# Gate matrices from two accumulated rounded products with a split gate value, and reordered joints in a hybrid attention and PEER block

## The reference

```python
xn = rms_norm(h); proj = xn @ w_in            # q, k, v of two branches, two gates
y_a = sliding_window_sink_attention(...)      # softmax whose denominator is sum(p) + exp(sink - m)
y_b = chunked_relbias_attention(...)
h += (sigmoid(g_a) * (y_a @ w_a) + sigmoid(g_b) * (y_b @ w_b)) @ w_out
# PEER: 8 heads, 128 + 128 sub-keys, 16 experts of 16384 for each head
qry = rms_norm(h) @ w_query
s1, s2 = qry[half 0] @ keys1.T, qry[half 1] @ keys2.T
v1, i1 = top_k(s1, 16); v2, i2 = top_k(s2, 16)
top_s, pos = top_k(all 256 sums v1 + v2, 16); idx = i1 * 128 + i2 at pos
gate = softmax(top_s)
act = gelu(xt . expert_down[idx]) * gate
h += sum over the 128 picked of act * expert_up[idx]
```

## Time and profile before

| | |
|---|---|
| median of 3 runs | 3632.18 us (3631.12 to 3638.24) |
| the profiled execution: its time, its span | 3641.5 us, 3639.7 us |
| mean granted TensorE clock | 0.992 |
| busy PE, weight loads (PEld) | 3552.3 us (98%), 3228.1 us |
| busy DVE, ACT, POOL | 2163.0 (59%), 1418.0 (39%), 2026.1 us (56%) |
| DMA | 871.95 MB, 240 GB/s over the span |
| chain that ended last, by engine | PE 83%, DVE 10%, DMA 3%, ACT 2% |
| chain, the two largest lines | PE L1507 76%, DVE L1300 4% |

### The profile page before, as it was taken

The page is one execution under the profiler, slowest core; times in us unless marked ns, Lnnn a source line. Parts: engine busy times, 40 slices in busy tenths (PEclk is TensorE's granted clock), DMA queues, the critical chain, the costliest instruction groups (busy, mean ns, idle before and its releaser), DMA issues.

```text
span 3639.7 us, 50829 instructions
## 1 busy us (share of the span) xinstructions
PE 3552.3 (98%) x20069; PEld 3228.1 (89%) x20069; DVE 2163.0 (59%) x3752; ACT 1418.0 (39%) x1782; POOL 2026.1 (56%) x696
## 2 busy tenths in 40 slices
PE   7999999999999999998999999999989999999999
PEld 5777777777788878898999999999989999999999
DVE  6444444344575138996666666533467777777774
ACT  5544545555422223323444434433333333333332
POOL 2333333333344434476666667676767777777774
PEclk9999999999999999999999999999999999999999
DMA  3322222222234322287888888889989999999994
GB/s 150 133 101 98 89 88 95 89 89 93 106 139 185 116 103 94 97 331 297 325 345 338 337 342 333 350 347 361 351 330 357 347 349 357 352 354 355 354 351 152
DMA packets 181721, 871.95 MB, mean 240 GB/s; under 512 B 15520, under 2 KB 69024, under 8 KB 90400
## 3 DMA queue, kind: packets, MB, share of 16 engines
q1 hardware_dynamic: 59376, 399.48, 29.6%
q0 software_dynamic: 46224, 336.61, 23.3%
q10 hardware_dynamic: 75936, 133.28, 10.0%
HBM read 805.32 MB, written 69.21 MB: 240 GB/s over the span
## 4 chain that ended last, share of the span: by engine, by line
PE 83%; DVE 10%; DMA 3%; ACT 2%; issue 1%; DVEq 1%; ACTq 0%; POOL 0%; SPq 0%
PE ps L1507 76%; DVE ps L1300 4%; PE ps L1737 2%; DMA g_exp<-g_dram 1%; PE ps L1588 1%; PE ps L1580 1%; PE ps L1570 1%; DVE h_dense L1427 1%; DMA expert_rows<-down_rows,idx 1%; DVE psm L1009 1%; PE ps L1523 1%; ACT w_hi L414 1%; DMA g_dram<-gate_buf 0%; DVE tk_i L1198 0%; DVE tk_i L1191 0%
## 5 line engine op out<-in xcount | busy, mean ns | idle before, releaser
L354 POOL TENSOR_TENSOR w_e_lo<-w_e_raw,w_e_hi 128x2048 fp32r<-128x2048 f32 x256 | 1185.0, 4630 | 537.7 <-ACT w_e_hi L720 536.3
L347 POOL TENSOR_TENSOR w_lo<-w_raw,w_hi 128x2048 fp32r<-128x2048 f32 x115 | 536.3, 4664 | 964.8 <-ACT w_hi L414 964.8
L1507 PE MATMUL ps<-act_hi,w_e_hi 128*128 128x352 f32 x2048 | 666.2, 325 | 14.6 <-DVE h_dense L1427 11.9
L1507 PE MATMUL ps<-sn_hi,w_e_hi 128*128 128x352 f32 x2048 | 670.3, 327 | 8.7 <-DVE sn_lo L1179 4.4
L1507 PE MATMUL ps<-act_lo,w_e_hi 128*128 128x352 f32 x2048 | 663.4, 324 | 0.0
L1507 PE MATMUL ps<-act_hi,w_e_lo 128*128 128x352 f32 x2048 | 662.5, 323 | 0.0
L1507 PE MATMUL ps<-sn_hi,w_e_lo 128*128 128x352 f32 x2048 | 660.2, 322 | 0.0
L1507 PE MATMUL ps<-sn_lo,w_e_hi 128*128 128x352 f32 x2048 | 658.6, 322 | 0.0
L720 ACT ACTIVATE w_e_hi<-w_e_raw 128x2048 fp32r<-128x2048 f32 x256 | 489.3, 1911 | 202.2 <-DMA w_e_raw<-w_stream 109.6
L1287 DVE SCALAR_TENSOR_TENSOR expert_rows<-expert_rows,ps 128x2048 f32<-128x2048 f32 x160 | 363.3, 2285 | 205.1 <-DMA expert_rows<-down_rows,idx 113.1
L1507 PE MATMUL ps<-xn_hi,w_hi 128*128 128x512 f32 x1088 | 447.4, 411 | 18.9 <-DVE xn_lo L924 18.9
(11 more groups left out here) (256 smaller groups left out, 4891.9 us busy)
## 6 DMA issues: line engine op xcount, KB each, us to landing
w_e_raw<-w_stream SPq DMA_DIRECT2D x256, 1024.0 KB
w_raw<-w_stream SPq DMA_DIRECT2D x116, 1024.0 KB, 4.8
gel_dram<-gel_all ACTq DMA_DIRECT2D x32, 704.0 KB
g_dram<-gate_buf ACTq DMA_DIRECT2D x11, 2048.0 KB
gel_in<-gel_dram ACTq DMA_DIRECT2D x32, 704.0 KB
g_exp<-g_dram ACTq DMA_DIRECT2D x32, 704.0 KB
gate_dram<-g_raw ACTq DMA_DIRECT2D x32, 256.0 KB, 2.0
g_in<-gate_dram ACTq DMA_DIRECT2D x16, 512.0 KB, 6.2
```

The lines of the kernel that those rows point to most:

```text
L347: nc.gpsimd.tensor_tensor(wlo[s][:, :], raw[s][:, :], whi[s][:, :].bitcast(F32), ALU.subtract).then_inc(lo_ready, 1)
L354: nc.gpsimd.tensor_tensor(e_lo[j % 4][:, :], e_raw[j % 4][:, :], e_hi[j % 3][:, :].bitcast(F32), ALU.subtract).then_inc(lo_ready, 1)
L1507: m = mm(ps[:, bank, 0:width], lhs[:, w], r, start=(n % (3 * per) == 0), stop=(n % (3 * per) == 3 * per - 1))
```

## The change

1. **Gate matrices.** `gt` is split into `gt_hi` (rounded, ACT) and `gt_lo` (the rest, DVE). DVE writes three one-hot matrices of a token instead of two, and PE accumulates two rounded products instead of one four-byte product. `turn_i2` on PE waits for `gt_lo`.
2. **Softmax A.** The sums of the scores and of the sink lie side by side in `sums`, and one reduction over them takes the place of the addition of L1009.
3. **Branch joint.** ACT waits for a quarter of the last attention block for each `y_hi`, not for all of it, and its rounding of the next weights and `take_gate` come later among them. DVE makes `y_lo` 0 to 6 before `attended(15)`, the others after it.
4. **Query joint.** DVE makes `hn_lo` by quarters, 0 to 11 before the last `residual`, and 12 to 15 after it.
5. **Down joint.** ACT rounds the second tile's weights (`peer_hi(1)`) first, then makes all 16 `sn_hi`, then `query_out`. DVE makes `sn_lo` before `top_of_heads(*others, 2)`.
6. **Dots.** Of rows 16 to 23 only 16 stays ahead of the softmax; 17 to 19 come after `tk_done` and 20 to 23 after `key_line`. FIRST_USED is later for the five groups after the first: 7, 10, 13, 15, 16 become 9, 11, 14, 16, 18.
7. **Loads.** The four parts of `h_dense` are issued one a tile in tiles 113 to 116, and `h_sparse` at group 16 of the up stage.

```diff
-FIRST_USED = [5, 7, 10, 13, 15, 16]
+FIRST_USED = [5, 9, 11, 14, 16, 18]
...
                     e = nc.scalar.activation(sc[:, hf, 0:n], sc[:, hf, 0:n], ACT.Exp, bias=negm[:, hf:hf + 1],
-                                             accum_out=psm[:, hf:hf + 1])
+                                             accum_out=sums[:, 2 * hf:2 * hf + 1])
...
-            act.wait_ge(quarters, 4 * B_BRANCH)
             for c in range(CT):
-                if c == 1:
+                if c == 7:
                     take_gate(B_EPI + 2, 1, 2, 31, 7)
-                if c == 4:
+                if c == 8:
                     hi(B_BRANCH, 1)
+                act.wait_ge(quarters, 4 * (B_BRANCH - 1) + c // 4 + 1)
...
-            for c in range(5):
-                scaled_hi(c)
             peer_hi(1)
-            for c in range(5, 10):
+            for c in range(CT):
                 scaled_hi(c)
             query_out(CT - 1, 1)
-            for c in range(10, CT):
-                scaled_hi(c)
             key_out(CT - 1)
...
-                    nc.scalar.activation(gt[:, :], ps[:, GB, 0:TD], ACT.Copy).then_inc(gthi_ready, 1)
+                    nc.scalar.activation(gt_hi[:, :], ps[:, GB, 0:TD], ACT.Copy).then_inc(gthi_ready, 1)
...
-                    for c in range(4):
-                        act.dma_start(h_dense[:, 4 * TD * c:4 * TD * (c + 1)], h_dense_dram[c]).then_inc(h_in, 16)
+                if T_FIRST < t <= T_FIRST + 4:
+                    c = t - T_FIRST - 1
+                    act.dma_start(h_dense[:, 4 * TD * c:4 * TD * (c + 1)], h_dense_dram[c]).then_inc(h_in, 16)
...
-            act.dma_start(h_sparse[:, :], h_sparse_dram).then_inc(h3_in, 16)
...
+                    if g == GROUPS // 2:
+                        act.dma_start(h_sparse[:, :], h_sparse_dram).then_inc(h3_in, 16)
...
                 if kind == "A":
-                    vec.tensor_tensor(psm[:, :], psm[:, :], esk[:, :], ALU.add)
+                    vec.reduce_sum(total[:, :], of_head, AX)
                     v.drain()
-                vec.reciprocal(rcp[:, :], psm[:, :]).then_inc(s_rcp, 1)
+                vec.reciprocal(rcp[:, :], total[:, :] if kind == "A" else of_head[:, :, 0]).then_inc(s_rcp, 1)
...
-            attended(15)
...
+            for c in range(7):
+                low_y(c)
+            attended(15)
+            v.drain()
+            for c in range(7, CT):
+                low_y(c)
...
-            v.wait_ge(quarters, 4 * B_QUERY)
-            low_h(0)
+            for c in range(12):
+                low_h(c)
             residual(CT - 1, 3)
-            for c in range(1, CT):
+            for c in range(12, CT):
                 low_h(c)
...
-            top_of_heads(*others, 2)
             for c in range(CT):
                 scaled_lo(c)
+            top_of_heads(*others, 2)
...
-            for j in range(16, FIRST_ROWS):
-                dot(j)
+            dot(16)
             v.wait_ge(tv_exp, 1)
...
+            for j in range(17, 20):
+                dot(j)
...
+            v.wait_ge(gthi_ready, 1)
+            vec.tensor_tensor(gt_lo[:, :], ps[:, GB, 0:TD], gt_hi[:, :].bitcast(F32), ALU.subtract).then_inc(gtlo_ready, 1)
...
+            for j in range(20, FIRST_ROWS):
+                dot(j)
...
-                    e = vec.tensor_scalar(g_oh[r][:, KEYS * t:KEYS * (t + 1)], key_line, i1_t[:, tok], gt[:, tok],
-                                          ALU.is_equal, ALU.mult)
+                    for g_part, gt_part in zip(g_oh[r], (gt_hi[:, tok].bitcast(F32), gt_lo[:, tok])):
+                        e = vec.tensor_scalar(g_part[:, KEYS * t:KEYS * (t + 1)], key_line, i1_t[:, tok], gt_part,
+                                              ALU.is_equal, ALU.mult)
...
-                pe.wait_ge(gthi_ready, 1)
+                pe.wait_ge(gtlo_ready, 1)
...
-                    m = mm(ps[:, GB, KEYS * t:KEYS * (t + 1)], oh2[r][:, KEYS * t:KEYS * (t + 1)],
-                           g_oh[r][:, KEYS * t:KEYS * (t + 1)], start=True, stop=True)
+                    for k, g_part in enumerate(g_oh[r]):
+                        m = mm(ps[:, GB, KEYS * t:KEYS * (t + 1)], oh2[r][:, KEYS * t:KEYS * (t + 1)],
+                               g_part[:, KEYS * t:KEYS * (t + 1)], start=(k == 0), stop=(k == 1))
```

More of the change, by code:

```diff
@@ L142, in build @@
         hn_x = at("hn_x", 181, D)
-        oh2 = [at(f"oh2_{s}", 165 + 2 * s, 512) for s in range(2)]
-        g_oh = [at(f"g_oh_{s}", 169 + 4 * s, 512) for s in range(2)]
+        oh2 = [at(f"oh2_{s}", 165 + 2 * s, 512, F32R) for s in range(2)]
+        g_oh = [[at(f"g_oh_{part}{s}", 169 + 4 * s + 2 * k, 512, F32R) for k, part in enumerate(("hi", "lo"))]
+                for s in range(2)]
         g_first = at("g_first", 177, 512)
@@ L166, in build @@
         eps_x, rstd_x = at("eps_x", 203, S), at("rstd_x", 205, S)
-        mx, negm, psm, esk, rcp = (at(n, 207 + k / 32, 2) for k, n in enumerate(["mx", "negm", "psm", "esk", "rcp"]))
+        mx, negm, total, rcp = (at(n, 207 + k / 32, 2) for k, n in enumerate(["mx", "negm", "total", "rcp"]))
+        sums = at("sums", 207.125, 4)
         neg_sink = at("neg_sink", 207.25, 16)
@@ L192, in build @@
         tv_sum, tv_rec = at("tv_sum", 206.5, 32), at("tv_rec", 206.625, 32)
-        gt = at("gt", 187, TD)
+        gt_hi, gt_lo = at("gt_hi", 187, TD, F32R), at("gt_lo", 188.5, TD)
         i1_t, i2_t = at("i1_t", 199, TD), at("i2_t", 201, TD)
@@ L257, in build @@
         root_ready = sem("h_rstd_columns")
-        gthi_ready, idx_ready = sem("gate_hi_ready"), sem("indices_ready")
+        gthi_ready, gtlo_ready, idx_ready = sem("gate_hi_ready"), sem("gate_lo_ready"), sem("indices_ready")
         oh_ready, g_mm, g_sb, g_dma = sem("one_hots"), sem("gates_mm"), sem("gates_sb"), sem("gates_stored")
@@ L457, in exps @@
                     e = nc.scalar.activation(sc[:, hf, 0:n], sc[:, hf, 0:n], ACT.Exp, bias=negm[:, hf:hf + 1],
-                                             accum_out=psm[:, hf:hf + 1])
+                                             accum_out=sums[:, 2 * hf:2 * hf + 1])
                 if kind == "A":
                     for hf in range(2):
-                        e = nc.scalar.activation(esk[:, hf:hf + 1], cols[:, bass.ds(C_SINK + 2 * a + hf, 1)], ACT.Exp,
+                        e = nc.scalar.activation(sums[:, 2 * hf + 1:2 * hf + 2], cols[:, bass.ds(C_SINK + 2 * a + hf, 1)], ACT.Exp,
                                                  bias=negm[:, hf:hf + 1])
@@ L479, in _ @@
             act.wait_ge(warm, 1)
-            nc.scalar.activation(esk[:, 0:1], negm[:, 0:1], ACT.Copy)
+            nc.scalar.activation(sums[:, 0:1], negm[:, 0:1], ACT.Copy)
             hi(B_PRE, 0)
@@ L1007, in step @@
                 v.wait_ge(s_exp, 4 * a + i + 1)
+                of_head = sums[:, :].rearrange("p (h c) -> p h c", h=2)
                 if kind == "A":
-                    vec.tensor_tensor(psm[:, :], psm[:, :], esk[:, :], ALU.add)
+                    vec.reduce_sum(total[:, :], of_head, AX)
                     v.drain()
-                vec.reciprocal(rcp[:, :], psm[:, :]).then_inc(s_rcp, 1)
+                vec.reciprocal(rcp[:, :], total[:, :] if kind == "A" else of_head[:, :, 0]).then_inc(s_rcp, 1)
             def attended(a):
@@ L1066, in _, with low_y @@
                 step("B", k, 15)
-            attended(15)
-            v.drain()
-            for c in range(CT):
+            def low_y(c):
                 v.wait_ge(yhi_ready, c + 1)
@@ L1127, in low_h @@
             def low_h(c):
+                v.wait_ge(quarters, 4 * (B_QUERY - 1) + c // 4 + 1)
                 v.wait_ge(hhi_ready, c + 1)
@@ L1366, in _ @@
             vec.tensor_copy(i2_t[:, :], ps[:, GB, 0:TD]).then_inc(idx_ready, 1)
-            v.wait_ge(gthi_ready, 1)
             v.drain()
```

## The result

The changed kernel takes 3589.54 us, the median of four runs (3583.95 to 3593.36), against 3633.71 us for the kernel before beside it: a ratio of 0.9876, with a 95% interval of 0.9857 to 0.9894, so 44.2 us less. Forecast were 3587 and 45.3 us less. A second set of runs gave 3588.83 us and 0.9868 (0.9854 to 0.9882), 47.2 us less.

A forecast was written before the change was run, and what follows sets the result against it. It took PE, busy for 98% of the span, as the bound, so only its work and gaps count. The terms summed to 45.3 us, taken off the median of 3632 to give 3587, with a range from 3545 to 3608.

The forecast's parts named there:

- softmax A: Attention softmax: a reduction in place of the addition ends all PE waits for ACT's scores, 12.7 us gained, low end 8.
- branch joint: Attention to branch: quarters remove PE's 7.0 us wait for y_lo and its 1.9 restart, 8.9 gained, ends 3 and 11.
- query joint: Before the query products: of 7.2 us for hn_lo and restart, 6.0 gained, 1.2 left for a collision; ends 3 and 8.7.
- down joint, top-k: Start of the down tiles, 1.2 us gained of 6.3; softmax of the top-k and its turn, 2 more, ends −4 and +16.
- gates: Gate products: eight rounded loads and passes cost what a round takes now, and the third one-hot fits on DVE: 0.
- loads: h_dense issued one a tile, 6.2 us gained; h_sparse moved to group 16, 8.3 gained after 3 taken off.
- 14.6 us wait at the turn: PE's wait at 1683.76: moving seven dots takes some 34 us off the chain, so wait and restart go, 16.5 gained.
- the chain that I named as next late: Top-k: late tv_sub delays ACT's rounding and POOL's 4.6 us for tile 16; PE waits 9 us, 11 with the restart.
- 10 us by the down joint: DVE's top-k of others queues behind the 16 sn_lo, so everything behind it, tv_sub too, comes about 10 us later.
- rival 1: Gates: rounded narrow products run at the rate of the columns, a round of 0.54, 31 us less, 3556; chance 0.11.
- The 0.89 us of the prediction's round: Gates: time of one round before the change, from its first record at 1725.37 to a wide product's load at 1726.26.
- its last sign: Gates: the prediction is wrong if PE waits for the one-hots.

The follow-up runs named there:

- e4: The kernel before with only the softmax change of attention A, a reduction over two sums in place of the addition: 3621.95 us, ratio 0.9961.
- e6: The kernel before with only the branch joint and the query joint by quarters: 3618.91 us, ratio 0.9961.
- e3: The changed kernel with the gate matrices as before, one four-byte product and two one-hots a token: 3586.46 us, ratio 0.9860.
- e5: The kernel before with only the moved loads, h_dense one part a tile and h_sparse at group 16: 3620.83 us, ratio 0.9957.

## Why the prediction was right, and where its steps were off

The forecast was 3587 us and the time 3589.5 and 3588.8. Term by term, forecast against measured:

```
                        forecast  measured
softmax A                   12.7  12.7 to 13.2, stage times (e4)
branch joint                 8.9  9.2, stage times (e6)
query joint                  6.0  7.5, stage times (e6)
down joint, top-k            3.2  6 to 8 (1.3 + 181.8, 1.3 + 181.0 against 3.6 + 171.8, 3.6 + 173.1)
gates                        0    -3, by intervals -10 to 4 (e3); -7 by stages
loads                       14.5  11 to 20 (e5)
```

The middles of the last column add up to 49 us, against 44.2 and 47.2 measured for the whole; the intervals of the gates and the loads hold the difference. So it is in part luck that the forecast of 45.3 came so close: the two joints and the top-k gave 5 to 7 us more than forecast, and the gates took some that the sum didn't have.

**Softmax A.** Right in place, mechanism and size. By the Trainium skill (SBUF — State Buffer, section "SBUF: two separate sides") a DVE operation with two SBUF inputs and a GpSimd operation that reads SBUF lock each other out of a shared pair of ports. The trace agrees: the reduction, with one, had 157 ns in the mean, where the addition had 944. The same collision was seen again in `y_lo`, 4.71 us beside POOL's 4.62.

**Joints.** Right: the collisions stay, behind PE's stock of chunks. The query joint gave 7.5 and not 6.0. Its remaining collision cost PE 0.6 us where I had left 1.2, and the restart was sized too small, 1.9 for 2.3; 0.5 us is not placed. One reading of the text is off: `y_lo` in the earlier trace rows didn't end with `w_lo` but 0.55 us after it (964.12 and 963.57), which is near the 0.68 that a `y_lo` takes by itself. So the collision held it for 4 us.

**Down joint and the top-k.** The 14.6 us wait at the turn went, as forecast, and the chain that I named as next late (`tv_sub`, ACT's exponential, `w_e_hi` and `w_e_lo` of tile 16) took its place, with 5.2 us where the text says 9. The step that failed is "10 us by the down joint": the run with DVE's order undone leaves `tv_sub` where it was. Counted from the first down product, the exponential that waits for it came after 120.9 and 120.7 us in the two executions of before and after 125.9 and 127.1 in those of the changed kernel, 5 to 6 us later and not 13 to 14. The gathers of rows 8 to 11, the "3 to 4 more" of the text, are 2 to 4 of these; the rest isn't placed. The waits for `sn_lo` (2.7) and `q_sb` (1.8, forecast 2.4) are there too. That the term came out at 6 to 8 us and not at 3.2 follows from the waits: `sn_lo` and the turn were 19.0 us before, and `sn_lo`, `q_sb`, `w_e_lo` and the first one-hots are 12.4 after.

**Gates.** Right that the round stays what it was: rounded products cost 0.11 us each, whether 128 columns move or 64, where the prediction had one row of another narrow product. The Trainium skill's rule that a load takes its number of columns over 1.2 GHz (TensorE: Matmul & The Clock Gate, section "LDWEIGHTS (loading the stationary operand)") gives an estimate of 107 ns. The 0.11 us agree with it.

The prediction says of the rule on four passes that it "isn't seen: the records show two passes". That reading is wrong. The Trainium skill states (FP8 and Floating Point Precision, section "TensorE Precision Notes") that a four-byte product takes four passes. The trace agrees at 512 columns: 0.87 us against 0.23, in two records, so a record isn't a pass. What fails in rival 1 is not this rule but the step from it to half a round, since a rounded product of 128 columns still costs its 0.11.

The 0.89 us of the prediction's round was also read to the wrong mark: the load at 1726.26 is that of the second wide product behind the gates. By the same mark the round is 0.89 after as well (1707.17 to 1708.06), and from product to product 0.84 in place of 0.81.

The third one-hot fitted: DVE is busy for 39.48 of 43.5 us in five tiles after (37.7 forecast). PE's waits for the one-hots are 3.0 us, all at the start. By its last sign, "if PE waits for the one-hots", the prediction would be wrong, though it takes off 3 us for just this place in another sentence; the run with two one-hots has the wait too (3.9), so it says nothing against the third. That the gates term was 0 is the weakest point: the stage table has it nearer to −7.

**Loads.** The sum is right, the reading behind it was too sure of one execution. The 9.4 us wait of the earlier trace rows isn't in every execution with the loads as they were: 9.4 and 1.3 in the two of before, 4.4 with the reduction alone, 1.3 with the joints alone. What I took off for a wait at group 16 (3 us) did not occur. So far as these two errors offset each other, that is luck.

**The step from profile to median.** I took the sum from the median as it stood. The profiled execution held more of the `g_exp` wait than the three others, so a part of the 9.3 us by which it lay over the median may have been in my sum, against what the prediction says ("not of what set that execution apart"). How large a part is open, since the executions with 1.3 us were the fastest of their runs, 12 and 9 us below their medians.

## What to carry to other kernels

Two operations that hold each other up needn't be kept apart; it is enough that the consumer has more work in hand than one collision lasts, which a wait by quarters gave here. A product with 128 stationary columns cost 0.11 us on TensorE at 128 and at 64 moving columns, so splitting a narrow four-byte product in two gained nothing, and only fewer products did (39.6 us for half of them, by the rounds). At 512 moving columns it would differ, by the rows above: 0.87 us for a four-byte product against 0.45 for two rounded ones. Before a wait that hangs on a transfer enters a sum, look at it in a second execution.

## What the runs showed of the hardware that wasn't expected

PE's rate in an unbroken stream at full clock differs between executions of the same kernel: 933 and 947 wide products in 150 us of the down stage, against 1057 and 1057 in 220 us of attention, where DMA moved 92 GB/s and not some 355. Over the 1080 us of the down tiles, 1.5% would be 16 us, an estimate, where the eight times of the changed kernel spread by 14.6. What sets it wasn't tried.
